# Block two's attention: value products ahead of turning, and the maximum ahead of the store

## What is computed

```python
for l in range(DEPTH):
    h = _rmsnorm(x, norm_g[l])
    z = h @ w_in[l]
    (nsa_q, nsa_kv, nsa_gate, nsa_silu, fox_qkv, fox_f, fox_silu, mem_q, mem_silu, merge_g) = _split(z, IN_SPLITS)
    o_a = _nsa(nsa_q, nsa_kv, nsa_gate, ...) * jax.nn.silu(nsa_silu)
    o_b = _fox(fox_qkv, fox_f, ...) * jax.nn.silu(fox_silu)
    mem_kv = _rmsnorm(mem, mem_norm_g[l]) @ w_mem_kv[l]
    o_m = _memory_xattn(mem_q, mem_kv, ...) * jax.nn.silu(mem_silu)
    g = jax.nn.sigmoid(merge_g).reshape(B, T, N_BRANCH, D)
    u = g[:, :, 0] * (o_a @ w_branch_a[l]) + g[:, :, 1] * (o_b @ w_branch_b[l]) + g[:, :, 2] * (o_m @ w_branch_m[l])
    x = x + u @ w_out[l]
```

## Time and profile before

| | |
|---|---|
| median of 3 runs | 3042.14 us |
| the profiled execution's own time | 3052.15 us |
| its span | 3050.7 us |
| TensorE matmul busy | 2998.7 us (98%) |
| VectorE busy | 1483.3 us (49%) |
| ScalarE busy | 803.5 us (26%) |
| GpSimd busy | 1936.4 us (63%) |
| attention of the first layer | about 1838 to 2080 us of the span |
| attention of the second layer | about 2560 to 2815 us |

### The profile page before, as it was taken

How to read it: one execution, slowest core, us unless ns; L and a number is a source line. 1 busy time by engine, 2 the same in 40 slices (tenths; PEclk the granted TensorE clock), 3 DMA queues, 4 the chain that set the end, 5 groups by cost and what they waited for, 6 DMA issues and landing times.

```text
span 3050.7 us, 41907 instructions
## 1 busy us (share of the span) xinstructions
PE 2998.7 (98%) x15546; PEld 2516.8 (82%) x15554; DVE 1483.3 (49%) x3007; ACT 803.5 (26%) x1751; POOL 1936.4 (63%) x2202
## 2 busy tenths in 40 slices
PE   9999999999999989999999999999999999999999
PEld 8888888888888878888888887888888887888887
DVE  1333334377740593877304746663233463664332
ACT  1111111232210342222103225662102213664110
POOL 5555555589987797999876762125777484222775
PEclk8999999999999999999999999999999899999999
DMA  4222222123232222222323231112333232111222
GB/s 142 102 88 90 92 92 86 62 79 98 97 100 97 76 83 70 97 97 97 116 97 126 90 97 43 29 36 70 97 115 114 85 109 70 36 43 34 91 97 90
DMA packets 70217, 261.48 MB, mean 86 GB/s; under 512 B 8320, under 2 KB 8832, under 8 KB 68224
## 3 DMA queue, kind: packets, MB, share of 16 engines
q1 hardware_dynamic: 65696, 232.81, 23.5%
q10 hardware_dynamic: 4320, 25.99, 2.3%
HBM read 251.43 MB, written 2.10 MB: 83 GB/s over the span
## 4 chain that ended last, share of the span: by engine, by line
PE 92%; DVE 3%; issue 2%; POOL 2%; ACT 1%; DMA 0%; ACTq 0%; POOLq 0%; DVEq 0%
PE bank L370 24%; PE bank L371 24%; PE bank L372 24%; PE bank L1895 3%; PE bank L1880 2%; PE bank L410 2%; PE bank L397 1%; PE bank L662 1%; PE bank L402 1%; PE bank L398 1%; PE bank L1861 1%; POOL w_lo L2247 1%; PE bank L1598 1%; PE bank L1306 1%; PE bank L634 1%
## 5 line engine op out<-in xcount | busy, mean ns | idle before, releaser
L2247 POOL TENSOR_TENSOR w_lo<-w_raw,w_hi 128x256 fp32r<-128x256 f32 x1736 | 1403.8, 839 | 36.2
L2243 POOL TENSOR_SCALAR w_hi<-w_raw 128x1024 fp32r<-128x1024 f32 x434 | 489.9, 1129 | 1047.3 <-PE bank L372 932.0
L370 PE MATMUL bank<-in_hi,w_hi 128*128 128x512 f32 x1408 | 555.3, 394 | 0.8 <-POOL w_lo L2247 0.5
L372 PE MATMUL bank<-in_hi,w_lo 128*128 128x512 f32 x1408 | 549.1, 390 | 0.0
L371 PE MATMUL bank<-in_lo,w_hi 128*128 128x512 f32 x1408 | 548.5, 390 | 0.0
L370 PE MATMUL bank<-z_hi,w_hi 128*128 128x512 f32 x976 | 392.4, 402 | 0.0
L372 PE MATMUL bank<-z_hi,w_lo 128*128 128x512 f32 x976 | 381.4, 391 | 0.0
L371 PE MATMUL bank<-z_lo,w_hi 128*128 128x512 f32 x976 | 380.8, 390 | 0.0
L372 PEld LDWEIGHTS bank<-in_hi,w_lo 128*128 128x128 f32 x1408 | 264.7, 188 | 56.1
L370 PEld LDWEIGHTS bank<-in_hi,w_hi 128*128 128x128 f32 x1408 | 264.9, 188 | 54.0 <-issue 0.9
L371 PEld LDWEIGHTS bank<-in_lo,w_hi 128*128 128x128 f32 x1408 | 265.0, 188 | 52.4
(11 more groups left out here) (436 smaller groups left out, 5103.0 us busy)
## 6 DMA issues: line engine op xcount, KB each, us to landing
w_raw<-in_units SPq DMA_DIRECT2D x434, 512.0 KB, 3.5
bias<-in_bias ACTq DMA_DIRECT2D x8, 1152.0 KB, 5.1
o_all<-in_cmp_w ACTq DMA_DIRECT2D x4, 2048.0 KB, 8.1
x_res<-in_x ACTq DMA_DIRECT2D x4, 512.0 KB, 9.1
mem_in<-in_mem ACTq DMA_DIRECT2D x2, 1024.0 KB, 8.6
nsa_q_hi<-nsa_q_hi SPq DMA_DIRECT2D x16, 128.0 KB, 2.3
nsa_q_lo<-nsa_q_lo SPq DMA_DIRECT2D x16, 128.0 KB, 2.3
out<-x_res ACTq DMA_DIRECT2D x4, 512.0 KB, 2.6
```

What stands on the lines that cost most here:

```text
L370: pe.matmul(out, hi[:, w], rh, start=start and n == 0, stop=False)
L372: last = pe.matmul(out, lo[:, w], rh, start=False, stop=stop and n == len(tiles) - 1)
L2243: d = c.s.unit_hi.on(pool.tensor_scalar(c.w_hi[s][:, :], c.w_raw[s][:, :], 1.0, 0.0, ALU.mult, ALU.add))
L2247: last = pool.tensor_tensor(c.w_lo[s][:, w], c.w_raw[s][:, w], c.w_hi[s][:, w].bitcast(F32), ALU.subtract)
```

## The change

It exchanges two calls in TensorE's step, and moves one call from the start of VectorE's step behind the maximum and the factors, ahead of the side work. No instruction is added, removed or resized.

```diff
@@ pe_attend @@
     for now in range(STEPS):
         if now < TASKS:
             pe_logits(pe, c, tasks[now])
+        if 0 <= now - 4 < TASKS:
+            pe_output(pe, c, tasks[now - 4])
         if 0 <= now - 2 < TASKS:
             pe_turn(pe, c, tasks[now - 2])
-        if 0 <= now - 4 < TASKS:
-            pe_output(pe, c, tasks[now - 4])
@@ dve_attend @@
     for now in range(STEPS):
-        if 0 <= now - 5 < TASKS:
-            dve_store(dve, c, tasks[now - 5])
         if now < TASKS:
             t = tasks[now]
             ...
@@
                 step.on(dve.tensor_scalar(sa[:, 10:11], sa[:, 8:9], c.gate[:, a.i, col:col + 1], None, ALU.mult), ("factor", a.t))
+        if 0 <= now - 5 < TASKS:
+            dve_store(dve, c, tasks[now - 5])
         n, r = divmod(now, CHUNK)
```

## The result

The changed kernel takes 3102.27 us (median of 4 runs, 3096.9 to 3112.43); the kernel before, in 4 runs beside it, 3044.48 (3040.51 to 3047.27). The ratio is 1.0195, with a 95% interval of 1.0165 to 1.0225: slower, as forecast, but by 58 us where the forecast had 32, and above the range's end of 3095. The profiled execution took 3112.43 (span 3111.0), the longest of its four; the one before, 3052.15.

The account below looks back on a forecast made before the run. TensorE, busy 98% of the span, was taken to bound the kernel. Losses at the places summed to 16.0 us a layer, 32 for two, added to the 3042 us median: 3074 us, range 3048 to 3095.

Parts of the forecast that it names:

- place A: Four-tile tasks from step 5 of a group: first turning 0.64 us later, three pairs of steps 0.4 to 0.5 us longer.
- The cycle: Two steps of four-tile tasks: store after exponential, release, products, turning, copy and next exponential sum to 3.40 us.
- steps 2 to 23 of the first group: Start of a layer: 0.4 us with no earlier delay, plus the losses of place D (1.3) and place C (1.05).
- place D: Steps 12 to 17, where no turning waited: new waits of 0.55 and 0.75 us, together 1.3, four times a layer.
- place C: Steps 21 to 25: the store ends later behind side work, reduction and factors; 1.05 us lost, four times a layer.
- places B and A: Between groups: 0.6 us for steps 27 to 31 after the query split, then 0.8 and 0.5; 1.9, three times.
- end of a layer: Layer's ends: 0.4 + 0.5 = 0.9 us lost in all, of which 0.5 at the end.
- The bounds: Lower: 34 old waits each 0.3 us longer, 10 us. Upper: all 128 pairs of steps lose 0.4, 51 us.
- The reduction's wait: VectorE: each reduction waits for the store right ahead; at most 0.08 us more, taken as inside the rounding.
- Products hide the wait: Rival: bank free in time, products cover turning's waits on the exponential; 17.4 us less, 3027 us. Chance 0.10.
- even: Rival: losses at old waits and the maximum found 0.20 us sooner cancel; 3042 us, within 6. Chance 0.12.
- The clock falls: Rival: more waits halve TensorE's clock in 20 us of each of eight groups; up to 160 us, 3230. Chance 0.02.

Follow-up runs that it names:

- E10: Kernel before, with the store last in every VectorE step and value products ahead of turning in odd steps alone (three or four key tiles): 3102.92 us, ratio 1.0195.
- E11: Kernel before, with the store last in every VectorE step and value products ahead of turning in even steps alone (one or two key tiles): 3072.05 us, ratio 1.009.
- E4: Kernel before, with value products ahead of turning and VectorE's step as reduction, maximum, store, reciprocal, gate: 3080.5 us, ratio 1.0128.
- E5: Kernel before, with value products ahead of turning and the store right behind the reduction, ahead of reciprocal, maximum and gate: 3060.34 us, ratio 1.0059.
- E1: Kernel before, with value products ahead of turning and the store left at the start of VectorE's step: 3049.36 us, ratio 1.0021.
- E3: Changed kernel with eight state buffers for six, so the reduction no longer waits for the store right ahead: 3098.97 us, ratio 1.0189 to the kernel before.
- E2: Kernel before, with only the store moved behind the gate in VectorE's step, turning still first: 3065.35 us, ratio 1.0078.
- E9: Kernel before, with value products ahead of turning and the store behind the reciprocal, ahead of the maximum: 3084.36 us, ratio 1.0134.
- E7: Kernel before, with only the maximum moved ahead of the reciprocal, store first and turning first as before: 3049.47 us, ratio 1.0023.

## Why the prediction was right in direction and short in size

**The mechanism held.** Products of s-4 need the store of s-6, which waits for the exponential of s-2. E10 and E11 show it at the long tasks, where the cycle of place A has it. Waits at L1895 for VectorE are 96, within the 40 to 100 forecast, 49.8 us for "30 us or more", and turning kept 4. That all catch up in a projection is seen in the stretches: from the second group on each loses the same in every group.

**The step that failed is the sum of the places**, 16.0 us a layer; the stretches have 27.9. Place by place, as forecast and as measured (changed less before, the first stretch without the clock):

```
                                  forecast              measured
steps 2 to 23 of the first group  0.4 + 1.3 + 1.05      1.7 + 2.9 = 4.6
place D, three times              1.3                   2.05
place C, three times              1.05                  1.70
places B and A, three times       1.9                   4.4, 3.6, 3.6
end of a layer                    0.5                   0.44
```

Every term but the end was too small, by a factor of 1.6 to 2.3. The end, 0.5, was worked out from no row, so that it came out is luck. (In place C the prediction's own rows give 1.14 us for step 21, where it says 1.2.) Three things were behind the rest.

*The cycle is longer than 3.40 us.* VectorE in the changed kernel at a place A (timeline):

```profile
1989.74 0.69 DVE L2052 TENSOR_TENSOR o_lo<-o_all,nsa_o_hi 128x512 fp32r<-128x512 f32 x1
1990.35 0.68 DVE L2047 TENSOR_TENSOR o_all<-bank,o_all 128x512 f32<-128x512 f32 x1
1990.95 0.28 DVE L1988 TENSOR_REDUCE at_st<-bank 128x1 f32<-128x128 f32 x1
1991.15 0.15 DVE L1996 RECIPROCAL at_st<-at_st 128x1 f32<-128x1 f32 x1
1991.27 0.21 DVE L2002 TENSOR_SCALAR at_st<-at_st,nsa_minus 128x1 f32<-128x1 f32 x1
1991.40 0.20 DVE L2013 TENSOR_SCALAR at_st<-at_st,gate_rows 128x1 f32<-128x1 f32 x1
1991.52 0.28 DVE L2066 SCALAR_TENSOR_TENSOR o_rows<-bank,at_st,o_rows 128x64 f32<-128x64 f32 x1
```

TensorE there:

```profile
1988.87 0.61 PE L1880 MATMUL bank<-ident,at_p 128*128 128x128 f32 x4
...
1991.94 1.07 PE L1895 MATMUL bank<-win_v,at_pt 128*128 128x64 f32 x8 [0.90 <-DVE o_rows L2066]
1992.85 0.61 PE L1880 MATMUL bank<-ident,at_p 128*128 128x128 f32 x4
```

ScalarE there:

```profile
1990.09 0.78 ACT L1919 ACTIVATE at_p<-bank,at_st,nsa_scale 128x512 f32<-128x512 f32 x1
1990.75 0.20 ACT L1919 ACTIVATION_READ_ACCUMULATOR at_p<-bank,at_st,nsa_scale 128x1 f32 x1
...
1993.50 0.60 ACT L1908 ACTIVATE at_pt<-bank 128x512 f32<-128x512 f32 x1 [0.91 <-PE bank L1880]
1993.99 0.77 ACT L1919 ACTIVATE at_p<-bank,at_st,nsa_scale 128x512 f32<-128x512 f32 x1
```

From turning to turning, 1988.87 to 1992.85, are 3.98 us. The three pairs that answer to those of the earlier trace rows take 3.70 (1985.17 to 1988.87), 3.98 and 3.70 (to 1996.55), 11.38 together for 9.77; the prediction had 10.2. Pair by pair, before had 2.40, 3.79 and 3.58: most of the 1.6 is lost in the first pair, at whose end TensorE had waited for nothing. Term by term, for the second: exponential over at 1990.95, store over at 1991.80, 0.85 for 0.64, because the reduction, held by side work, starts only at 1990.95 and stands ahead of the reciprocal. From the store's end to the products 0.14 for 0.05: I had taken ScalarE's release of TensorE for VectorE's. Products to turning 0.91 for 0.84, as they now start from a standstill. Turning to copy, 1992.85 to 1993.50, 0.65 for 0.49 + 0.04: the copy waits for the last turning to land, and in the old order I had read the start of the next work of TensorE for it. Copy to exponential 0.49 for 0.48, exponential 0.86 (1990.09 to 1990.95) for 0.86. Together 3.90.

*A second coupling was missed.* The prediction tied the store to the exponential alone. It stands behind the reduction as well, and so behind the logits of s-1 and the side work ahead of it. E4 shows that this path, with a maximum in it and no exponential of the same step, gives 38 of the 58 us (32 of some 55 at equal clock), and E5 that a bare reduction gives 13 more than E1 (10 at equal clock).

*The parts were priced at the old waits' places.* I counted loss where the trace of before had waits or VectorE was visibly late. That the store's place had slack in the other steps, which the change used up, is my reading; the record shows only that they lose too. The first group lost the most, 4.6 and 4.4 us, where a later one loses 2.05 + 1.70 and 3.6.

**The bounds.** The upper one, 128 pairs of steps at 0.4 us, 51 us, was no bound, since 0.4 was a size and not a limit: 56 us by waits are 0.44 a pair. The three pairs at place A lose 1.3, 0.2 and 0.1. That nearly every stretch loses, which I took for the far end, is what happened.

**The reduction's wait** for the store right ahead was taken as 0.08 us at most. It is 0.18 us a time (0.38 for 0.20) and, by E3, nothing in the total. The Trainium skill (VectorE: DVE Perf Modes, The DRAIN you can't avoid) has it that a semaphore adds nothing; the total agrees here, the starts do not. Another section of that page (Two Vector instructions with no wait between them) has an instruction that it calls held start only once all before it have finished; but what it calls held goes by the partitions at which operands start, not by semaphores, so it doesn't settle which row is the later. The rows do: 0.38 is behind the store's 0.28, 0.20 is not.

**The rivals.** *Products hide the wait* and *even* are out: the products were late themselves. E1 is the case of the first rival at its best, the bank freed as early as before, and loses 7 us. So its premise, that the products are ready to cover the wait, fails on TensorE's own side. *The clock falls* came true in small, see the last section. Its 3230 is the forecast of 3074 plus 160, not the 3042 before plus 160, which is 3202; and the 1.4 us wait that it leans on stands at 1849.38, outside the window of the earlier trace rows, though the granted clock is 1.00 there too.

## What to carry to other kernels

Before a piece of work is put under another's wait, ask when its own output bank comes free, and follow the freeing instruction through everything ahead of it in its engine's queue, the side work and the reduction for the newest tile included. If that chain holds the wait that is to be covered, the exchange closes a cycle, and it then turns at the length of the whole chain in every step, not only where waits stood before. Price a wait by the starts of the matmuls around it, not by the idle time listed: in place C each listed wait cost some 0.16 us more.

## What the runs showed of the hardware

**Release times.** From the end of a VectorE store that frees a bank to the start of the matmul that writes it: 0.14 us (1991.80 to 1991.94 in the changed kernel, 1972.58 to 1972.72 in E4), and 0.15, to the rounding, at every wait of the changed kernel's list at L1895 for a store. From an exponential of ScalarE to turning it was 0.05, at all 34 waits of the kernel before.

**The clock.** The changed kernel's profile has a stretch at the start of its first attention in which the clock fell (columns: us, busy us of PE, PEld, DVE, ACT and POOL, granted clock, DMA share, GB/s):

```profile
1840.00:1850.00 10.00, 8.80 (x53) 7.36 (x53) 4.79 (x17) 3.94 (x15) 4.62 (x7) 1.00 0.17 53
1850.00:1860.00 10.00, 8.55 (x39) 7.08 (x39) 5.88 (x27) 6.41 (x17) 1.98 (x3) 0.61 0.15 53
1860.00:1870.00 10.00, 9.82 (x51) 7.36 (x51) 5.32 (x24) 4.88 (x16) 0.00 (x0) 0.71 0.01 2
```

A mean of 0.61 means that for most of those 10 us the clock stood at its lower level, 1.2 GHz, and for the rest at 2.4. What TensorE did ahead of it, in the timeline:

```profile
1849.87 0.33 PE L1880 MATMUL bank<-ident,at_p 128*128 128x128 f32 x1 [0.44 <-ACT at_p L1919]
...
1852.33 1.11 PE L1880 MATMUL bank<-ident,at_p 128*128 128x128 f32 x4 [1.32 <-ACT at_p L1919]
```

The four turnings at 1852.33 last 1.11 us where others last 0.61. The kernel before has a wait of up to 1.4 us and keeps 1.00 in these windows. It has a fall of its own elsewhere, between the attentions (0.69 from 2360 to 2380), which the changed kernel's profile has not. In those 20 us TensorE was busy for 20.00. So I can't say that these waits cause the fall, only that one came with them. There are falls in the first stretch of both layers of the changed kernel (0.70 and 0.71) and of the second of E10 (0.71), none in the first of E10, whose stretches are the same from then on, and none in E1, E2, E9 and E11. E7 has one in its second layer (0.83), and there the products stand behind turning and the store is first, as before. So the waits at the products are not what it takes.

By the first stretch a fall costs 3.6 us (23.07 for 19.44, first layer of the changed kernel and of E10; the two layers of E10 itself have 19.44 and 23.25), against the 20 us a group that the rival in the prediction had. The granted clock of the change's four runs was 0.989, 0.993, 0.997 and 0.994, their times in the same order 3112.43, 3104.12, 3096.9 and 3100.43. The kernel before took 3040.3 to 3040.5 in its runs at 0.997, so at equal clock the change costs 56 us there, as much as the stretches say. The clock is a small part of the 58.

Also open: whether a third output bank, which would part the store from the products, would let the exchange win. That wasn't tried.
